# Seven block products for eight in the feed-forward down products of a two-block transformer kernel

## The chip, the cores and the metric

The kernel runs on one NeuronCore of a Trainium2 chip. The core has a matrix engine (TensorE, PE in the profile, with its weight loads as PEld), three engines for the rest (VectorE is DVE, ScalarE is ACT, GpSimd is POOL), and a SyncE queue (SP) that starts the transfers from HBM. The engines run their own instruction streams and meet at semaphores. The metric is the device time of one launch in microseconds, the median of the runs.

## The reference

Two layers of one transformer block, then one block of another kind, for 512 tokens of width 1024, in float32. The change lies in the feed-forward part of the first two layers:

```python
h2 = rms_norm(x, norm2[l])                                        # x: 512 x 1024
x = x + jnp.square(jax.nn.relu(h2 @ w_up[l])) @ w_down[l]         # w_up: 1024 x 4096, w_down: 4096 x 1024
```

In front of it in a layer stand a projection, four kinds of attention and an output projection. Behind the second layer comes a modulated block, whose modulation is the sum over k of `c[k] * w_ada[k, :]`, 3072 wide; VectorE forms it during the second layer's feed-forward part.

## The kernel before

**Precision.** TensorE takes float32 operands in a rounded format (float32r). Each operand is split into a high part (the rounded value) and a low part (value minus high part), and each product of two tiles is three matmuls, high x high, high x low, low x high (`three`, L2136 to L2138). A matmul takes a 128 x 128 stationary tile and a moving tile of 512 columns.

**Weights.** A job is 1024 rows by 512 columns of a weight matrix, in two halves ("pieces") of 512 x 512, 1 MB each. SP loads a piece into one of four `raw` slots, ScalarE copies it to `w_hi` (L1413), GpSimd subtracts to make `w_lo` in two instructions of 128 x 1024 (L1367). `w_hi` and `w_lo` have two slots: the piece after next can be split only when TensorE has finished with the slot.

**Feed-forward part.** The 4096 hidden columns come in four groups of 1024. A group has four jobs: two "up" jobs make the hidden values transposed (hidden feature on the partitions, 512 tokens along the free dimension) in the four PSUM banks G, a tile of 128 features in each; then two "down" jobs with the hidden values as stationary and a piece of `w_down` as moving operand make 512 tokens x 512 columns in G. A job is 96 matmuls, a half job 48; a group is 384. For each up tile ScalarE takes the relu out of PSUM (L1693), VectorE squares it (L2087), makes the high part (L2088) and the low part (L2089), all 128 x 512. For each down tile VectorE adds the bank, scaled by the inverse square norm `inv_square`, to X in SBUF (L2068). In the second layer VectorE also adds six parts of the modulation in a group (L2115, 128 x 1024 each). The loop over groups is a hardware loop on most engines, and each engine's order within it is written out by hand; nothing reorders an engine's instructions.

**Around it.** Before the first group the X rows are turned through the PSUM banks S and split; behind the last group the next layer's first job does the same. The S banks are free during the feed-forward part.

## Time and profile before

| | us |
|---|---|
| median of 3 runs (1829.14 to 1831.54) | 1830.73 |
| profiled execution, first to last instruction | 1830.6 |
| TensorE busy | 1790.4 |
| VectorE busy | 932.7 |
| GpSimd busy | 728.6 |
| ScalarE busy | 663.0 |

The profile covers one execution. Of its own time the record gives the span from the first to the last instruction, and nothing around it. Busy times are sums over an engine's instructions. Matmuls overlap in the pipeline, so their durations add up to more than the time that they need; the distance of their starts is the cost of one. In a timeline row the first number is the start in us, the second the duration; a bracket at the end says how long the engine stood idle before, and what ended that.

### The profile page before, as it was taken

How to read it: one execution, taken by the hardware profiler on the slowest of the kernel's cores; microseconds unless marked ns; L12 is line 12 of the kernel's file. 1: busy time of each engine (PE TensorE's matmuls, PEld its weight loads, DVE VectorE, ACT ScalarE, POOL GpSimd, SP SyncE). 2: the span in 40 equal slices, each digit the busy share in tenths (PEclk: the TensorE clock that was granted, in tenths of full speed). 3: DMA queues.
4: the chain of work that ended last, by engine and by line, in shares of the span. 5: the costliest groups of instructions: out<-in, count | busy, mean ns of one | idle time of the engine just before them, and what ended most of it. 6: DMA issues, size and time to landing. Idle time of an engine off the chain costs nothing.

```text
span 1830.6 us, 22975 instructions
## 1 busy us (share of the span) xinstructions
PE 1790.4 (98%) x9055; PEld 1461.3 (80%) x9057; DVE 932.7 (51%) x1500; ACT 663.0 (36%) x1234; POOL 728.6 (40%) x328
## 2 busy tenths in 40 slices
PE   8999899999999999999999999999999999999998
PEld 8677668888888886776688888888788988888786
DVE  4678752514232246797627362727522134339476
ACT  4543653312222245345523131222435343443213
POOL 4232434444444533333444444544343434224343
PEclk9999999999999999999999999999899999999999
DMA  7225002222232232220025524242232223222221
GB/s 233 70 69 172 2 24 92 93 92 92 95 111 92 69 98 97 69 70 1 24 69 185 179 97 161 92 161 96 93 133 86 70 75 116 87 69 92 93 69 46
DMA packets 105023, 171.00 MB, mean 93 GB/s; under 512 B 21679, under 2 KB 39495, under 8 KB 103784
## 3 DMA queue, kind: packets, MB, share of 16 engines
q1 hardware_dynamic: 103896, 169.79, 28.2%
q8 instruction: 60, 0.98, 0.2%
q14 instruction: 27, 0.22, 0.0%
q10 hardware_dynamic: 1040, 0.00, 0.0%
HBM read 166.56 MB, written 7.93 MB: 95 GB/s over the span
## 4 chain that ended last, share of the span: by engine, by line
PE 90%; DVE 6%; ACT 2%; issue 1%; DMA 0%; SPq 0%; DVEq 0%; ACTq 0%
PE G L2136 26%; PE G L2138 25%; PE G L2137 25%; PE S L2423 2%; PE S L1138 1%; DVE select L1976 1%; PE G L2459 1%; DVE work L1812 1%; DVE neg_max L2012 1%; PE S L2184 1%; PE S L1112 1%; DVE top L1811 1%; PE G L2407 1%; PE S L1123 1%; PE G L2440 1%
## 5 line engine op out<-in xcount | busy, mean ns | idle before, releaser
L1367 POOL TENSOR_TENSOR w_lo<-raw,w_hi 128x1024 fp32r<-128x1024 f32 (+2 forms) x268 | 658.5, 2478 | 976.1 <-ACT w_hi L1413 667.0
L2136 PE MATMUL G<-h_hi,w_hi 128*128 128x512 f32 x896 | 355.9, 397 | 1.9 <-DVE h_lo L888 1.9
L1413 ACT ACTIVATE w_hi<-raw 128x2048 fp32r<-128x2048 f32 (+1 forms) x94 | 178.9, 1903 | 492.7 <-PE G L2138 492.7
L2138 PE MATMUL G<-h_hi,w_lo 128*128 128x512 f32 x896 | 349.9, 391 | 0.0
L2137 PE MATMUL G<-h_lo,w_hi 128*128 128x512 f32 x896 | 349.7, 390 | 0.0
L2136 PE MATMUL G<-w_hi,h_hi 128*128 128x512 f32 (+2 forms) x704 | 277.2, 394 | 2.2 <-DVE h_lo L1765 1.2
L2138 PE MATMUL G<-w_hi,h_lo 128*128 128x512 f32 (+2 forms) x704 | 267.1, 379 | 0.0
L2137 PE MATMUL G<-w_lo,h_hi 128*128 128x512 f32 (+2 forms) x704 | 266.7, 379 | 0.0
L2136 PEld LDWEIGHTS G<-h_hi,w_hi 128*128 128x128 f32 x896 | 168.5, 188 | 39.2 <-issue 4.4
L2138 PE MATMUL G<-w_hi,u_lo 128*128 128x512 f32 x512 | 199.2, 389 | 0.0
L2136 PE MATMUL G<-w_hi,u_hi 128*128 128x512 f32 x512 | 199.2, 389 | 0.0
L2137 PE MATMUL G<-w_lo,u_hi 128*128 128x512 f32 x512 | 199.2, 389 | 0.0
L2138 PEld LDWEIGHTS G<-h_hi,w_lo 128*128 128x128 f32 x896 | 168.6, 188 | 36.2
L2137 PEld LDWEIGHTS G<-h_lo,w_hi 128*128 128x128 f32 x896 | 168.7, 188 | 34.6 <-issue 1.0
L2136 PEld LDWEIGHTS G<-w_hi,h_hi 128*128 128x128 f32 x704 | 140.1, 199 | 31.8 <-issue 11.9
L2138 PEld LDWEIGHTS G<-w_hi,h_lo 128*128 128x128 f32 x704 | 140.0, 199 | 21.2
L2137 PEld LDWEIGHTS G<-w_lo,h_hi 128*128 128x128 f32 x704 | 140.3, 199 | 20.3 <-issue 1.9
L2068 DVE SCALAR_TENSOR_TENSOR X<-G,inv_square,X 128x512 f32<-128x512 f32 x64 | 47.2, 749 | 210.5 <-PE G L2138 210.1
L2087 DVE TENSOR_TENSOR square<-relu 128x512 f32<-128x512 f32 x64 | 57.5, 899 | 158.1 <-ACT relu L1693 154.7
L722 ACT ACTIVATE w_hi<-raw 128x2048 fp32r<-128x2048 f32 x38 | 72.7, 1912 | 120.6 <-PE G L2138 120.6
L2138 PEld LDWEIGHTS G<-w_hi,u_lo 128*128 128x128 f32 x512 | 96.1, 188 | 20.0
L2137 PEld LDWEIGHTS G<-w_lo,u_hi 128*128 128x128 f32 x512 | 96.1, 188 | 20.0
(325 smaller groups left out, 2232.4 us busy)
## 6 DMA issues: line engine op xcount, KB each, us to landing
raw<-in_w_in_dram SPq DMA_DIRECT2D x40, 1024.0 KB, 5.2
raw<-in_w_up_dram SPq DMA_DIRECT2D x32, 1024.0 KB, 5.1
raw<-in_w_down_dram SPq DMA_DIRECT2D x32, 1024.0 KB, 5.0
raw<-in_w_out_dram SPq DMA_DIRECT2D x12, 1024.0 KB, 4.9
w_ada<-in_w_ada_dram SPq DMA_DIRECT2D x4, 3072.0 KB, 11.8
skew_scratch<-line_scratch SPq DMA_DIRECT2D x1, 4608.0 KB
raw<-in_w_in_dram SPq DMA_DIRECT2D x8, 512.0 KB, 4.1
raw<-in_w_in_dram SPq DMA_DIRECT2D x4, 832.0 KB, 6.6
```

Source lines behind the costliest of these rows:

```text
L722: act.activation(w_hi[:, c % SPLIT_SLOTS], raw[:, c % RAW_SLOTS], ACT.Copy).then_inc(high_ready, 1)
L1112: ins = pe.matmul(dst, queries[at, tile0 + n, q], keys[at, tile0 + n, k], start=True, stop=True)
L1123: ins = pe.transpose(S[:, 2 * (it % 2) + e, P * b:P * b + P], prob2[:, it % 2, e, P * b:P * b + P], ident)
L1138: ins = pe.matmul(dst, prob2[:, it % 2, e, P * place:P * place + P], values[:, m + 1 - blocks + b, HD * h:HD * h + HD], start=b == 0, stop ...
L1367: ins = pool.tensor_tensor(w_lo[:, c % SPLIT_SLOTS, part, 0:n], raw[:, c % RAW_SLOTS, part, 0:n], w_hi[:, c % SPLIT_SLOTS, part, 0:n].bitc ...
L1413: act.activation(w_hi[:, c % SPLIT_SLOTS, :, 0:n], raw[:, c % RAW_SLOTS, :, 0:n], ACT.Copy).then_inc(high_ready, 1)
L2068: dve.scalar_tensor_tensor(dst, G[:, t, :], factor, dst, ALU.mult, ALU.add).then_inc(bank_drained, 1)
L2087: step.done(dve.tensor_tensor(square[:], relu[:, n % 2, :], relu[:, n % 2, :], ALU.mult))
L2136: pe.matmul(dst, a_hi, b_hi, start=first, stop=False)
L2137: pe.matmul(dst, a_hi, b_lo, start=False, stop=False)
L2138: return pe.matmul(dst, a_lo, b_hi, start=False, stop=last)
L2423: pe.matmul(bank, qkT[at, p % 2, q, P * qt:P * qt + P], qkT[at, p % 2, k, P * tiles[0]:P * (qt + 1)], start=True, stop=False)
```

## The change

The product of a group, hidden (512 tokens x 1024) by down weights (1024 x 1024), is cut into 2 x 2 blocks (A11 to A22 of the hidden values with 256 tokens x 512 features, B11 to B22 of the weights with 512 x 512) and formed with seven block products in Winograd's form of Strassen's algorithm: A11·B11, A12·B21, S2·T2, S3·T3, S1·T1, S4·B22, A22·T4, with sums S1 = A21 + A22, S2 = S1 - A11, S3 = A11 - A21, S4 = A12 - S2 and four sums T of weight blocks. A product is 24 matmuls (two token tiles, four feature tiles, three each).

TensorE's order in groups 0 to 2 is A11, A12, S2, S3, U0, S1, U1, S4, A22, U2, U3, where U0 to U3 are the half jobs of the next group's up products; the last group has the seven products alone. The products use two bank pairs of S. A11, S2, S3 and A22 add up in the "long" pair, S1 and S4 in the short one (which A12 has before them); VectorE reads a pair after each product, 14 sums in a group, and the next product on that pair waits for it.

VectorE now makes the four S, two of the T (T2, T3), the low parts of the hidden blocks, and the low parts of the weights of five products, in place of square and high part. GpSimd makes the low parts of the up halves as before, those of S4's and A22's weights, and T1 and T4. ScalarE squares, makes all high parts (weights in halves of 128 x 1024). A fifth raw slot is added, and each slot's role moves from group to group. The modulation's weights come in 24 loads of 128 x 1024 into one buffer instead of four of 128 x 6144. The group loops are unrolled.

The core of the diff (removed lines are the group functions of the engines, told above):

```diff
+PRODUCTS = (("A11", "B11"), ("A12", "B21"), ("S2", "T2"), ("S3", "T3"), ("S1", "T1"), ("S4", "B22"), ("A22", "T4"))
+LONG_BANK = (True, False, True, True, False, False, True)
+READ_BEFORE = (P_A22, P_S4, P_A11, P_S2, P_A12, P_S1, P_S3)
+GOES_TO = ((0, 1, None), (0, 1, P_A11), (0, 0, None), (1, 0, None), (1, 0, P_S3), (0, 0, P_S2), (1, 1, None))
+def ffn_pieces():
+    order = [("U", 0, n) for n in range(4)]
+    for g in range(FFN_GROUPS):
+        more = g + 1 < FFN_GROUPS
+        for p in range(NP):
+            order.append(("P", g, p))
+            if more:
+                order += {P_S3: [("U", g + 1, 0)], P_S1: [("U", g + 1, 1)],
+                          P_A22: [("U", g + 1, 2), ("U", g + 1, 3)]}.get(p, [])
+    return order
...
 # SP, loads for group g during the products of g - 1
+                for g in range(1, FFN_GROUPS):
+                    sums = 2 * (l * FFN_GROUPS + g)
+                    wait_product_split(sp, l, g - 1, P_S2)
+                    sp.wait_ge(sum_made["T1"], sums)
+                    sp.wait_ge(sum_made["T4"], sums)
+                    load_up(g, 0)
+                    wait_product_split(sp, l, g - 1, P_S3)
+                    load_up(g, 1)
+                    load_modulation(1)
+                    wait_up_split(sp, l, g, 0)
+                    load_up(g, 2)
+                    wait_product_split(sp, l, g - 1, P_S1)
+                    load_up(g, 3)
+                    load_modulation(3)
+                    wait_up_split(sp, l, g, 1)
+                    load_down(g, "B11")
+                    wait_product_split(sp, l, g - 1, P_S4)
+                    load_down(g, "B12")
+                    load_modulation(1)
+                    wait_product_split(sp, l, g - 1, P_A22)
+                    load_down(g, "B22")
+                    wait_up_split(sp, l, g, 2)
+                    load_down(g, "B21")
+                    load_modulation(1)
...
 # GpSimd
+                    wait_product_split(pool, l, g, P_A11)
+                    weights_sum(g, "T1", role_slot(l, g, "B22"), role_slot(l, g, "B11"), t2_half)
+                    wait_product_split(pool, l, g, P_A12)
+                    weights_sum(g, "T4", role_slot(l, g, "B21"), role_slot(l, g, "B21"), t2_half)
+                    more = g + 1 < FFN_GROUPS
+                    if more:
+                        up_low(g + 1, 0)
+                        up_low(g + 1, 1)
+                    late_weight_low(g, P_S4)
+                    late_weight_low(g, P_A22)
+                    if more:
+                        up_low(g + 1, 2)
+                        up_low(g + 1, 3)
...
 # ScalarE
+                def products_high(g):
+                    at = lambda p: FFN_AT["P", g, p]
+                    more, last = g + 1 < FFN_GROUPS, l == DEPTH - 1
+                    up_tile(g, 1, 3)
+                    weight_half(at(P_A12), 0)
+                    block_high(g, "A12", 1)
+                    weight_half(at(P_A12), 1)
+                    block_high(g, "S2", 1)
+                    weight_high(at(P_S2))
+                    block_high(g, "A22")
+                    block_high(g, "S1")
+                    weight_high(at(P_S3))
+                    block_high(g, "S4")
+                    if more:
+                        up = lambda n: FFN_AT["U", g + 1, n]
+                        weight_high(up(0))
+                        weight_high(at(P_S1))
+                        weight_high(up(1))
+                        weight_high(at(P_S4))
                         for t in range(TT):
+                            up_tile(g + 1, 0, t)
+                        weight_high(at(P_A22))
+                        weight_high(up(2))
+                        first_blocks_high(g + 1)
+                        weight_high(up(3))
+                        second_blocks_high(g + 1)
+                        return
...
 # VectorE, group g
+                    more = g + 1 < FFN_GROUPS
+                    sums_s1_s2(g, 1)
+                    weight_low(g, P_A12, 0)
+                    block_low(g, "A12", 1)
+                    weight_low(g, P_A12, 1)
+                    take_sum(g, P_A11, 0)
+                    sum_s4(g)
+                    take_sum(g, P_A11, 1)
+                    block_low(g, "S2", 0)
+                    weight_low(g, P_S2, 0)
+                    block_low(g, "S2", 1)
+                    weight_low(g, P_S2, 1)
+                    take_sum(g, P_A12, 0)
+                    weight_low(g, P_S3, 0)
+                    take_sum(g, P_A12, 1)
+                    weight_low(g, P_S3, 1)
+                    block_low(g, "A22")
+                    if more:
+                        add_modulation(1)
+                    block_low(g, "S1")
+                    block_low(g, "S4")
+                    take_sum(g, P_S2, 0)
+                    if not more:
+                        weight_low(g, P_S1, 0)
+                    take_sum(g, P_S2, 1)
+                    if not more:
+                        weight_low(g, P_S1, 1)
+                    take_sum(g, P_S3, 0)
+                    if more:
+                        weight_low(g, P_S1, 0)
+                    take_sum(g, P_S3, 1)
+                    if more:
+                        weight_low(g, P_S1, 1)
+                        add_modulation(3)
+                    take_sum(g, P_S1, 0)
+                    take_sum(g, P_S1, 1)
+                    if more:
+                        add_modulation(1)
+                        for hh in range(2):
+                            sum_s3(g + 1, hh)
+                    take_sum(g, P_S4, 0)
+                    take_sum(g, P_S4, 1)
+                    if more:
+                        first_blocks_low(g + 1)
+                    take_sum(g, P_A22, 0)
+                    take_sum(g, P_A22, 1)
+                    if more:
+                        add_modulation(1)
+                        sum_t3(g + 1)
+                        sum_t2(g + 1)
+                        before_products(g + 1)
...
 # TensorE
+                def down_product(g, p):
+                    a = PRODUCTS[p][0]
+                    s = FFN_AT["P", g, p] % SPLIT_SLOTS
+                    hi, lo = high_of[a], low_of[a]
+                    for hh in range(2):
+                        wait_product_split(pe, l, g, p, hh)
+                        pe.wait_ge(act_low[a], blocks_upto(a, l, g) + (0 if a in WHOLE else hh) + 1)
+                        for r in range(2):
+                            bank = S[:, 2 * LONG_BANK[p] + r, :]
+                            if hh == 0:
+                                before = READ_BEFORE[p]
+                                if before < p:
+                                    wait_taken(pe, l, g, before, r)
+                                elif g:
+                                    wait_taken(pe, l, g - 1, before, r)
+                            at = slice(P * r, P * r + P)
+                            for kk in (2 * hh, 2 * hh + 1):
+                                ins = three(bank, hi[:, kk, at], lo[:, kk, at], w_hi[:, s, kk, :], w_lo[:, s, kk, :],
+                                            kk == 0 and (p == P_A11 or not LONG_BANK[p]) and p != P_S4,
+                                            kk == HALF_K - 1, p in CONTINUES)
```

`before_products(g)` makes the low parts of A11's weights, the first halves of S1 and S2 and the low part of A12's first half; it stands in front of group g, during U3. `weight_low`, `weight_half`, `up_low` and `late_weight_low` work on 128 x 1024, `sums_s1_s2` and `block_low` with a half on 128 x 512, whole blocks and `sum_s4` on 128 x 1024.

## Rows read from the trace of the kernel before

**Rows 1.** Part 1 of the page: busy us (share of the span) x instructions, by engine.
```profile
PE 1790.4 (98%) x9055; PEld 1461.3 (80%) x9057; DVE 932.7 (51%) x1500; ACT 663.0 (36%) x1234; POOL 728.6 (40%) x328
```

**Rows 2.** Stretch: us, PE, PEld, DVE, ACT, POOL busy, PEclk, DMA share, GB/s.
```profile
409.00:496.00 87.00, 87.00 (x386) 72.06 (x385) 26.09 (x32) 19.92 (x16) 39.58 (x17) 1.00 0.29 97
```

**Rows 3.** Timeline of TensorE and GpSimd in that layer: start us, duration us.
```profile
452.89 0.39 PE L2136 MATMUL G<-w_hi,u_hi 128*128 128x512 f32 x1
453.80 0.39 PE L2137 MATMUL G<-w_lo,u_hi 128*128 128x512 f32 x1
...
463.25 4.74 POOL L1367 TENSOR_TENSOR w_lo<-raw,w_hi 128x1024 fp32r<-128x1024 f32 x2 [6.13 <-ACT w_hi L1413]
474.13 4.75 POOL L1367 TENSOR_TENSOR w_lo<-raw,w_hi 128x1024 fp32r<-128x1024 f32 x2 [6.14 <-ACT w_hi L1413]
```

**Rows 4.** Groups of ScalarE by form: count | busy us, mean ns | idle before.
```profile
L1413 ACT ACTIVATE w_hi<-raw 128x2048 fp32r<-128x2048 f32 x90 | 172.5, 1916 | 492.7 <-PE G L2138 492.7
L1693 ACT ACTIVATE relu<-G 128x512 f32<-128x512 f32 x64 | 38.3, 599 | 114.0 <-PE G L2138 73.5 <-DVE u_lo L2089 40.5
L1413 ACT ACTIVATE w_hi<-raw 128x1680 fp32r<-128x1680 f32 x4 | 6.4, 1610 | 0.0
```

**Rows 5.** Timeline of VectorE in the first layer's feed-forward part.
```profile
440.68 0.69 DVE L2087 TENSOR_TENSOR square<-relu 128x512 f32<-128x512 f32 x1
441.41 0.43 DVE L2088 CAST u_hi<-square 128x512 fp32r<-128x512 f32 x1
...
453.17 0.75 DVE L2068 SCALAR_TENSOR_TENSOR X<-G,inv_square,X 128x512 f32<-128x512 f32 x1 [10.60 <-PE G L2138]
```

**Rows 6.** Timeline of GpSimd and VectorE in the second layer's feed-forward part.
```profile
1001.03 2.39 POOL L1367 TENSOR_TENSOR w_lo<-raw,w_hi 128x1024 fp32r<-128x1024 f32 x1 [6.25 <-ACT w_hi L1413]
1003.38 2.84 POOL L1367 TENSOR_TENSOR w_lo<-raw,w_hi 128x1024 fp32r<-128x1024 f32 x1
...
1001.06 2.91 DVE L2089 TENSOR_TENSOR u_lo<-square,u_hi 128x512 fp32r<-128x512 f32 x1
1003.90 3.41 DVE L2115 SCALAR_TENSOR_TENSOR ada_sum<-w_ada,c_col,ada_sum 128x1024 f32<-128x1024 f32 x1
1008.67 1.28 DVE L2115 SCALAR_TENSOR_TENSOR ada_sum<-w_ada,c_col,ada_sum 128x1024 f32<-128x1024 f32 x1
...
1033.11 4.75 POOL L1367 TENSOR_TENSOR w_lo<-raw,w_hi 128x1024 fp32r<-128x1024 f32 x2 [6.14 <-ACT w_hi L1413]
...
1033.90 0.75 DVE L2068 SCALAR_TENSOR_TENSOR X<-G,inv_square,X 128x512 f32<-128x512 f32 x1 [12.90 <-PE G L2138]
```

**Rows 7.** Stretches, columns as in rows 2 (PEclk is the granted clock).
```profile
205.00:217.00 12.00, 10.03 (x93) 7.70 (x91) 10.40 (x22) 7.75 (x23) 3.98 (x4) 1.00 0.01 1
853.00:860.00 7.00, 5.94 (x43) 4.82 (x44) 6.83 (x16) 3.51 (x13) 2.51 (x2) 0.76 0.01 2
...
1303.00:1310.00 7.00, 7.00 (x37) 5.12 (x36) 4.85 (x16) 1.79 (x7) 0.00 (x0) 0.72 0.00 1
...
1316.00:1320.00 4.00, 4.00 (x14) 3.06 (x13) 2.33 (x5) 2.65 (x3) 0.98 (x1) 0.57 0.89 305
1320.00:1323.00 3.00, 3.00 (x17) 2.43 (x16) 1.75 (x2) 0.78 (x1) 3.00 (x2) 1.00 0.00 0
```

**Rows 8.** Timeline of TensorE at its longest gaps inside the span.
```profile
209.18 0.33 PE L2459 MATMUL G<-probT,rows_v 128*64 128x128 f32 x2 [1.77 <-ACT mixT_da L1621]
...
854.06 0.66 PE L2459 MATMUL G<-probT,rows_v 128*64 128x128 f32 x8 [1.77 <-ACT mixT_da L1621]
...
1315.35 0.47 PE L2136 MATMUL G<-h_hi,w_hi 128*128 128x512 f32 x1 [1.88 <-DVE h_lo L888]
...
1317.25 0.63 PE L2136 MATMUL G<-h_hi,w_hi 128*128 128x512 f32 x1
1317.68 0.63 PE L2137 MATMUL G<-h_lo,w_hi 128*128 128x512 f32 x1
```

**Rows 9.** Transfers by line: count, KB each, median us from issue to landing.
```profile
raw<-in_w_up_dram SPq DMA_DIRECT2D x32, 1024.0 KB, 5.1
```

More of the change, by code:

```diff
@@ L351 @@
               JOB_D: (D_COLS,), JOB_V: (CV_COLS, DV_COLS)}
-def loads_upto(c):
-    parts = [len(PROJ_PARTS[x // 2]) if x // 2 < PROJ_JOBS else 1 for x in range(c + 1) if x % RAW_SLOTS == c % RAW_SLOTS]
-    return 16 * sum(parts)
 FIRST_GROUP_PIECE = 2 * FFN_JOB
-LOADS_TO_GROUPS = [loads_upto(FIRST_GROUP_PIECE - RAW_SLOTS + s) for s in range(RAW_SLOTS)]
-GROUP_LOADS = 16 * 2 * GROUP_JOBS // RAW_SLOTS
-LAYER_LOADS = [x + FFN_GROUPS * GROUP_LOADS for x in LOADS_TO_GROUPS]
+MORE_RAW = RAW_SLOTS
+ROLES = ("B11", "B12", "B22", "B21", "T2")
@@ new lines, with raw_slot, role_slot, up_slot @@
+RAW_ORDER, RAW_ROLES = raw_places()
+def raw_slot(l, c):
+    return RAW_ORDER[l][c % RAW_SLOTS]
+def role_slot(l, g, role):
+    return RAW_ROLES[FFN_GROUPS * l + g][role]
+def up_slot(l, g, n):
+    return RAW_ORDER[l][n] if g == 0 else role_slot(l, g - 1, ("T2", "B12", "T2", "B11")[n])
+def product_slot(l, g, p):
+    role = PRODUCTS[p][1]
+    return role_slot(l, g, {"T3": "B12", "T1": "B11", "T4": "B21"}.get(role, role))
+def ffn_loads(l):
+    order = [("U", 0, n) for n in range(4)] + [("B", 0, role) for role in ROLES[:4]]
+    for g in range(1, FFN_GROUPS):
+        order += [("U", g, n) for n in range(4)] + [("B", g, role) for role in ROLES[:4]]
+    return order
@@ new lines, in load_slot, with count_loads, add @@
+def load_slot(l, what):
+    kind, g, n = what
+    return up_slot(l, g, n) if kind == "U" else role_slot(l, g, n)
+def count_loads():
+    counts, at = [0] * (RAW_SLOTS + 1), {}
+    def add(key, slot, parts=1):
+        counts[slot] += 16 * parts
+        at[key] = counts[slot]
+    for l in range(DEPTH):
+        for c in range(FIRST_GROUP_PIECE):
+            add((l, c), raw_slot(l, c), len(PROJ_PARTS[c // 2]) if c // 2 < PROJ_JOBS else 1)
+        for what in ffn_loads(l):
+            add((l, what), load_slot(l, what))
+    for c in range(TOTAL_PIECES - PIECE0):
+        add((DEPTH, c), raw_slot(DEPTH, c))
+    return at
@@ L1277, in _ @@
                 for c in range(FIRST_GROUP_PIECE):
-                    job, half, slot = c // 2, c % 2, c % RAW_SLOTS
-                    slot_free(number + (c + 1))
+                    job, half, slot = c // 2, c % 2, raw_slot(l, c)
+                    if l and c < RAW_SLOTS:
+                        wait_raw_free(sp, l - 1, c)
+                    else:
+                        slot_free(number + (c + 1))
                     if job < PROJ_JOBS:
@@ L2121, in _, with first_blocks_low @@
+                def first_blocks_low(g):
+                    for a in ("A11", "S3"):
+                        for hh in range(2):
+                            block_low(g, a, hh)
+                if last:
                     dve.wait_ge(c_loaded, 16)
@@ L2508, in _ @@
+                for kind, g, n in FFN_ORDER:
+                    (up_half if kind == "U" else down_product)(g, n)
             second_tensor(pe, three, product, in_rows, in_columns, turn)
```

605 lines of the change are left out of this document (422 added, 183 removed).

## The prediction

> **What bounds the kernel now.** The page first: TensorE is busy for 98% of the span, no other engine for more than 51% (weight loads, PEld, overlap the matmuls) [rows 1]. A stretch of 87 us, one feed-forward group of the first layer, has TensorE busy without a gap, VectorE 26 us, ScalarE 20 us, GpSimd 40 us [rows 2]. Busy time misleads as a cost of one matmul: the records last 390 ns, but overlap; the starts are 0.227 us apart [rows 3]. GpSimd's splits, one for each half job of 48 matmuls, start 10.88 us apart, which is 48 x 0.2267. A group of 8 half jobs is therefore 87.04 us [rows 3]. TensorE waits for nothing there [rows 2], so a matmul taken away is worth 0.2267 us, as long as the other engines keep up with the shorter products.
>
> **What is removed.** A group's down products need 7 x 24 = 168 matmuls for 192: 24 x 0.2267 = 5.44 us less, for 8 groups 43.5 us. Nothing else in the change gives time. A product now lasts 5.44 us, its halves 2.72 us, and what the old order had 10.88 us for must be done in that.
>
> **What the other engines get.** Their prices:
> - VectorE, both inputs in SBUF: 0.69 us for 512 wide when undisturbed [rows 5]. 1024 wide is not shown for a subtraction; it lies between the 1.28 us of a three-operand instruction [rows 6] and, at the least, 2 x 0.43 of a cast; I take 1.25, next to the same kind of operands. 0.05 between two.
> - Taking a sum from PSUM: 0.75 [rows 5].
> - ScalarE: 1.92 for 2048 wide and 1.61 for 1680 [rows 4] make 0.83 ns a column and 0.22 fixed, so 1.07 for 1024 and 0.64 for 512; a relu from PSUM 0.60 [rows 4].
> - GpSimd: 4.74 for two of 1024 [rows 3], so 2.37 each. A signal between engines: about 0.1.
>
> In a group VectorE gave 8 x (0.69 + 0.43 + 0.69) = 14.5 us of such work and 6.0 of sums. Now: ten halves of weight low parts, four of T2 and T3 and four whole blocks (S4; the low parts of A22, S1, S4) at 1.25, and six S halves and eight low halves at 0.69, together 32 us, and 14 sums, 10.5 us. In the second layer 6 modulation parts, as before. GpSimd keeps 16 pieces: eight of up weights, four late low parts, T1 and T4: 38 us.
>
> The sum of VectorE, 43 us in 81.6, fits. But the two engines exclude one another, and the trace shows how [rows 6]. The low part started at 1001.06 takes 2.91 us, because GpSimd runs to 1003.42; GpSimd's next one, 2.84 for 2.37, waits for that low part; the modulation at 1003.90 takes 3.41 for 1.28, because GpSimd has the turn again. A sum from PSUM at 1033.90 in the middle of a GpSimd piece takes its 0.75: only work with all its inputs in SBUF is shut out. So each GpSimd piece inside a queue of VectorE's costs that queue what is left of the piece.
>
> **The path: VectorE's queue between the last up half and the third sum.** Zero is the end of U3, the products have ideal starts A11 0, A12 5.44, S2 10.88, S3 16.32, U0 21.76. S3 adds into the banks of S2, so its first matmul waits for the first sum of S2 (READ_BEFORE), and that sum stands on VectorE behind everything listed here.
> - ScalarE: relu and square of the last tile end at 1.45, then half a weight of A12 (2.55), A12's second half (3.2), the other weight half (4.3).
> - VectorE: S1 and S2 halves 1.55 to 2.97; weight low 4.3; A12 low 5.04; weight low 6.35. Product A12 needs these at 5.44 and 8.16: no stall. Sum of A11, 7.15.
> - At 6.45 GpSimd begins T4 (it waits for the A12 weight split) and holds until 8.8. S4 on VectorE runs 8.85 to 10.1; second sum of A11 10.95; T4's second piece 10.1 to 12.5 shuts out the low part of S2. Then low 13.2, weight 14.5, low 15.25, weight 16.55.
> - So S2 starts at 14.6 instead of 10.88, and ends at 20.05.
> - VectorE goes on: sum of A12 17.35, weight of S3 18.65, sum 19.45, weight 20.75, A22 low 22.05, S1 low 23.35. The load of U0 is issued when the weights of S2 are split, 16.6, and lands 5.1 us later [rows 9]; ScalarE 22 to 23.05; GpSimd wants its piece at 23.1, gets it at 23.35 and holds until 25.7. S4 low 26.95, first sum of S2 27.75.
> - S3 starts at 27.85 instead of 16.32: 11.5 us late, two idle gaps of TensorE, 3.7 and 7.8.
>
> In groups 0 to 2 of the second layer a modulation part stands behind A22's low part: 1.25 and one more GpSimd piece in front of S4's low part: S3 starts at 31.35, 15.0 late. In group 3 no up half follows, and GpSimd is out of the way: S3 starts at 25.5, 9.2 late, and 0.75 more for its second bank, whose sum waits behind half a weight split: 9.9. In the second layer two products with the gain stand there too, 1.7: 11.6. Sum: 3 x 11.5 + 9.9 + 3 x 15.0 + 11.6 = 101.0 us.
>
> Behind S3 there is slack. U0's low parts are ready 4 us ahead. S1 and S4 have an up half of 10.88 in front of them. A22 gets its first half 0.4 ahead. U2's second half is about even: GpSimd has A22 and U2 back to back, while VectorE puts low parts of the next A11 between; between 0 and 1.2 late, I take 0.6, for 6 groups 3.6 us. In the second layer SP's queue stands on the modulation's single buffer until VectorE has used it (three loads in a row between its U3 and B11 loads), but the next load behind it, B11, is wanted only after U3's split, some 30 us on. At the layer's end the sums in PSUM take 0.75 after the last matmul, as now: nothing.
>
> **The clock.** TensorE's clock fell where it had little to do: in 1303 to 1310, among thin matmuls, 0.72 was granted (it has two levels, 1.2 and 2.4 GHz, so over half of the time at the lower one), and behind a gap of 1.88 the matmuls start 0.43 apart instead of 0.227 [rows 7, 8]; 1316 to 1320 has 0.57, so 0.86 of those 4 us at the lower level, 3.4 us [rows 7]. Slow work of 3.4 to 4 us, say 3.7, loses 3.7 x (1 - 0.227/0.428) = 1.74 us. Around a gap of 1.77 that ends at 854.06, 0.76 was granted in 7 us; around the same gap, ended at 209.18, 1.00 [rows 7, 8]: so a fall after a gap is not certain. I take one of 1.74 for each S3 gap, 8 x 1.74 = 13.9; a slow S2 costs nothing, since VectorE is later anyway. Without any it is 0; with twice the length 28.
> The Trainium skill ("TensorE: Matmul & The Clock Gate", section "HAM oscillation — how this bites in real kernels") says that a wait which recurs in each round of the loop lets every round start at the lower clock. The rows leave this open, by them alone one could enter nothing or a half; so by the rule the sum is the one below, by the rows alone down to 14 us less.
>
> **Sum.** -43.5 + 101.0 + 3.6 + 13.9 = +75.0 us. The profiled execution took 1830.6 us between first and last instruction, the runs' median is 1830.73: the same. 1830.6 + 75 = 1905.6, I say **1906 us**, own range 1890 to 1925.
>
> **Rivals.**
> - *The pieces of GpSimd fall beside VectorE's queue.* The order of work leaves T4 and U0 free to come a few us earlier or later. Without the lock the queue is 5 x 0.69 + 10 x 1.25 + 5 x 0.75 and 19 gaps, 20.7 us; from 1.55 on S2's first sum ends at 22.2, S3 starts at 22.3, still 6.0 late; with the same additions as above 3 x 6.0 + 6.75 + 3 x 7.25 + 8.45 = 55.0. 1830.6 - 43.5 + 55.0 + 13.9 = 1856; without a fall of the clock 1842. For it: T4 comes from a wait, its start may slip. Against it: T4's wait is the very weight split that VectorE ends, so it falls in the queue by itself. Chance 0.19.
> - *The clock stays down longer,* for all of S3 and half of U0, about 11 us at half rate each time: 11 x 0.47 = 5.2 us for 1.74, and U2 late by 1.2: 1906 + 8 x 3.4 + 4 = 1937. For it: low grants from 1303 to 1320; against it: the full grant right behind, with dense work [rows 7]. Chance 0.12.
> - *The queue is short enough: faster.* The place is the same wait of S3 for the first sum of S2, the price is the 1024-wide instruction. If it goes at the cast's rate (0.86) and the lock doesn't strike, the ten save 3.9 us, S3 starts at 18.4, 2.1 late; 8 x 2.1 + 3 x 1.25 and 3.2 of the groups 3 = 24; 1830.6 - 43.5 + 24 = 1811. It decides from the point where S3 starts before 21.76, 5.44 behind the ideal. Against it: 0.69 for the two-input form, 0.43 for the cast alone [rows 5]. Chance 0.10.
> - Between these, at 1827 to 1834: chance 0.04. Forecast: 0.55.
>
> **Numbers.** A difference under 0.2% (3.7 us) is about what can't be told from none. Slower 0.55 + 0.19 + 0.12 = 0.86, same 0.04, faster 0.10. The range leaves out the two cases that aren't slower, 0.14, and half of the slow-clock case, 0.06: from the lower end of the first rival, 1842, to 1930.
>
> **What would show it.** 192 matmuls fewer, and TensorE idle before the first matmul of S3 in each group, 5 to 11 us, ended by VectorE's sum; a shorter gap before S2, ended by its low parts; both in all 8 groups, longest in the second layer's first three. VectorE's 1024-wide subtractions at 1.25 where GpSimd rests and 2.5 to 3.6 where it runs. Granted clock under 1 behind the gaps. I am wrong if S3 follows S2 without a gap, or if gaps stand before up halves.

## The result, and the profile after

The changed kernel takes 1883.66 us (median of 4 runs, 1881.34 to 1885.56), the kernel before beside it 1831.13 (1829.14 to 1833.9): a ratio of 1.0292, 95% interval 1.0276 to 1.0308. So it is slower, as forecast, and 22 us less slow than the 1906 that stood there: within the range of 1842 to 1930, below the 1890 to 1925 that the forecast itself had. The profiled span is 1883.8 against 1830.6, 53.2 more.

Part 1 of the page of the changed kernel answers to [rows 1]:

```profile
PE 1780.6 (95%) x8863; PEld 1441.2 (77%) x8865; DVE 1105.1 (59%) x1612; ACT 815.3 (43%) x1498; POOL 743.7 (39%) x328
```

The 192 matmuls are gone (9055 to 8863), and TensorE is idle for 103 us where it was idle for 40. Where it waits is read from the timeline of TensorE, rows with an idle time in the bracket: in the first layer's first group ahead of S2 and of S3, and in the second layer's first group ahead of A11 and of S3 (shorter ones, of 1.96 and 1.88 us, stand there ahead of A12 and S2):

```profile
367.34 0.50 PE L2633 MATMUL S<-w_hi,s_high 128*128 128x512 f32 x1 [2.32 <-DVE w_lo L2506]
376.83 0.47 PE L2633 MATMUL S<-w_hi,s_high 128*128 128x512 f32 x1 [2.12 <-DVE X L2535]
...
1022.81 0.80 PE L2633 MATMUL S<-w_hi,a_high 128*128 128x512 f32 x1 [13.63 <-DVE w_lo L2506]
...
1052.51 0.77 PE L2633 MATMUL S<-w_hi,s_high 128*128 128x512 f32 x1 [4.91 <-DVE X L2535]
```

The first two are the pair that was forecast: S2 waits for VectorE's low part of its weights, S3 for the first sum of S2 (X). They stand in every group, but in the first layer's groups 0 to 2 they are 2.3 and 2.1 us, not 3.7 and 7.8; in the others 1.9 to 3.4 and 2.5 to 4.9. The third was not forecast. Stretches of the same kernel, columns as in [rows 2]:

```profile
354.00:383.00 29.00, 24.56 (x100) 19.53 (x99) 23.58 (x23) 14.46 (x17) 10.95 (x4) 0.94 0.29 82
...
1009.00:1061.00 52.00, 29.62 (x99) 22.85 (x99) 38.37 (x34) 18.41 (x25) 17.57 (x6) 0.77 0.33 101
1121.00:1154.00 33.00, 26.28 (x101) 20.75 (x100) 26.19 (x26) 14.57 (x18) 12.65 (x5) 0.90 0.33 101
```

In 354 to 383 the kernel before had 29.00 us of TensorE at clock 1.00. The second layer loses more, and with the clock at 0.77 and 0.90.

The lengths of the groups come from the starts of their first A11 matmul. An ideal group is 87.04 - 5.44 = 81.6 us, the last one of a layer 7 x 5.44 = 38.1.

| | measured excess | forecast |
|---|---|---|
| first layer, groups 0 to 2 | 7.0 each (353.98, 442.60, ...: 88.6 apart) | 11.5 + 0.6 + 1.74 = 13.8 each |
| first layer, group 3 | 9.3 (619.80 to 667.22) | 9.9 + 1.74 = 11.6 |
| second layer, group 0 | 30.8 (1009.02 to 1121.39) | 15.0 + 0.6 + 1.74 = 17.3 |
| second layer, groups 1 and 2 | 11.5 and 11.1 | 17.3 each |
| second layer, group 3 | 10.8 | 11.6 + 1.74 = 13.3 |
| elsewhere | 2.1 (1.7 ahead of the first group, 0.4 between the layers) | 0 |
| matmuls | -43.5 | -43.5 |
| sum | +53.1 (the spans: +53.2) | +75 |

VectorE and GpSimd from A11's first matmul (353.98) on, where the forecast had laid out its queue:

```profile
359.70 0.75 DVE L2535 SCALAR_TENSOR_TENSOR X<-S,inv_square,X 128x512 f32<-128x512 f32 x1
360.36 3.00 DVE L2473 TENSOR_TENSOR hidden<-hidden,s_sum 128x1024 f32<-128x1024 f32 x1
363.39 0.75 DVE L2535 SCALAR_TENSOR_TENSOR X<-S,inv_square,X 128x512 f32<-128x512 f32 x1
364.06 2.09 DVE L2498 TENSOR_TENSOR s_low<-s_sum,s_high 128x512 fp32r<-128x512 f32 x1
366.08 1.21 DVE L2506 TENSOR_TENSOR w_lo<-raw,w_hi 128x1024 fp32r<-128x1024 f32 x1
367.21 0.68 DVE L2498 TENSOR_TENSOR s_low<-s_sum,s_high 128x512 fp32r<-128x512 f32 x1
367.81 1.21 DVE L2506 TENSOR_TENSOR w_lo<-raw,w_hi 128x1024 fp32r<-128x1024 f32 x1
...
372.54 1.21 DVE L2498 TENSOR_TENSOR a_low<-hidden,a_high 128x1024 fp32r<-128x1024 f32 x1
373.67 1.21 DVE L2498 TENSOR_TENSOR s_low<-hidden,s_high 128x1024 fp32r<-128x1024 f32 x1
374.81 1.21 DVE L2498 TENSOR_TENSOR s_low<-hidden,a_high 128x1024 fp32r<-128x1024 f32 x1
375.94 1.39 DVE L2535 SCALAR_TENSOR_TENSOR X<-S,inv_square,X 128x512 f32<-128x512 f32 x2
...
359.86 5.74 POOL L1669 TENSOR_TENSOR raw<-raw 128x1024 f32<-128x1024 f32 x2 [8.21 <-DVE w_lo L2506]
375.40 5.21 POOL L1651 TENSOR_TENSOR w_lo<-raw,w_hi 128x1024 fp32r<-128x1024 f32 x2 [9.79 <-ACT w_hi L1766]
```

The reader sees three things. T4 (L1669) falls into the queue where it was put, at 5.9 us after A11's start (forecast 6.45), and shuts out S4 (3.00 for 1.21) and the first low part of S2 (2.09 for 0.68), but not the sum from PSUM at 363.39 (0.75 as always). U0's piece (L1651) comes at 375.40, after VectorE's last low part has begun, so its lock strikes nothing that S3 waits for. And where nothing shuts VectorE out, its instructions start 1.13 and 0.60 us apart, less than the 1.21 and 0.68 that they are recorded with; the forecast had 1.30 and 0.74.

### The profile page after: what moved, and what is told of

It is laid out like the page before. It is cut to its first block, busy times and chain, and to the rows that moved or that the text cites. A ratio compares the mean times of both kernels' runs of the same rounds, so it can differ in the third digit from the quotient of the medians.

```text
span 1883.8 us, 22625 instructions
## 1 busy us (share of the span) xinstructions
PE 1780.6 (95%) x8863; PEld 1441.2 (77%) x8865; DVE 1105.1 (59%) x1612; ACT 815.3 (43%) x1498; POOL 743.7 (39%) x328
## 4 chain that ended last, share of the span: by engine, by line
PE 72%; DVE 16%; POOL 4%; issue 3%; ACT 3%; DMA 1%; SPq 1%; DVEq 0%; ACTq 0%
PE G L2633 18%; PE G L2635 18%; PE G L2634 18%; POOL w_lo L1651 3%; DVE w_lo L2506 2%; PE S L2633 2%; PE S L2634 2%; PE S L2635 2%; PE S L2921 2%; DVE hidden L2473 2%; POOL w_lo L1660 2%; DVE s_low L2498 1%; PE S L1344 1%; DVE X L2535 1%; DVE select L2349 1%
## 5 line engine op out<-in xcount | busy, mean ns | idle before, releaser
L1616 POOL TENSOR_TENSOR w_lo<-raw,w_hi 128x1024 fp32r<-128x1024 f32 (+2 forms) x140 | 335.2, 2415 | 581.5 <-ACT w_hi L930 297.2
L1766 ACT ACTIVATE w_hi<-raw 128x1024 fp32r<-128x1024 f32 x140 | 144.1, 1052 | 269.3 <-PE G L2635 154.8
L1651 POOL TENSOR_TENSOR w_lo<-raw,w_hi 128x1024 fp32r<-128x1024 f32 x52 | 138.9, 2693 | 184.7 <-ACT w_hi L1766 184.7
L2535 DVE SCALAR_TENSOR_TENSOR X<-S,inv_square,X 128x512 f32<-128x512 f32 x112 | 82.4, 744 | 111.4 <-PE S L2635 110.8
L2633 PE MATMUL S<-w_hi,s_high 128*128 128x512 f32 x192 | 84.8, 442 | 45.6 <-DVE X L2535 24.3
L2633 PE MATMUL S<-w_hi,a_high 128*128 128x512 f32 x256 | 101.7, 397 | 16.4 <-DVE w_lo L2506 15.6
L2635 PE MATMUL S<-w_hi,s_low 128*128 128x512 f32 x256 | 106.7, 417 | 0.0
L1632 POOL TENSOR_TENSOR prob<-prob,inv_sum 128x256 f32<-128x256 f32 (+3 forms) x48 | 60.1, 1253 | 106.8 <-DVE inv_sum L2390 106.4
L2634 PE MATMUL S<-w_lo,a_high 128*128 128x512 f32 x256 | 101.1, 395 | 0.0
```

The costliest lines, as they stand in the source:

```text
L1616: ins = pool.tensor_tensor(w_lo[:, c % SPLIT_SLOTS, part, 0:n], raw[:, raw_slot(l, c), part, 0:n], w_hi[:, c % SPLIT_SLOTS, part, 0:n].bit ...
L1632: pool.tensor_tensor(part, part, inverse, ALU.mult).then_inc(prob_scaled, 1)
L1651: pool.tensor_tensor(w_lo[:, f % SPLIT_SLOTS, part], raw_at(up_slot(l, g, n))[:, part], w_hi[:, f % SPLIT_SLOTS, part].bitcast(F32), ALU.s ...
L1766: act.activation(w_hi[:, f % SPLIT_SLOTS, part], piece_source(l, FFN_ORDER[f])[:, part], ACT.Copy).then_inc(ffn_high, 1)
L2535: dve.scalar_tensor_tensor(X[:, t, at], S[:, 2 * LONG_BANK[p] + r, :], inv_square[:, t:t + 1], X[:, t, at], ALU.mult, ALU.add).then_inc(su ...
L2633: pe.matmul(dst, a_hi, b_hi, start=first, stop=False, skip_group_check=more)
```

## The experiments

My theory: the two gaps come from the order of VectorE's queue and from T4's lock on it, and the second layer adds its modulation. Rivals: VectorE has too much work in this stretch whatever its order; the clock is what costs; the second layer's excess is something else. Times of before beside these runs lie between 1829.3 and 1830.7; ratios are to them.

**1. The sums of S2 ahead of the low parts of S1, A22 and S4.**

```diff
                     weight_low(g, P_S3, 1)
+                    take_sum(g, P_S2, 0)
+                    take_sum(g, P_S2, 1)
+                    block_low(g, "S1")
...
                     block_low(g, "A22")
...
-                    block_low(g, "S1")
                     block_low(g, "S4")
-                    take_sum(g, P_S2, 0)
...
-                    take_sum(g, P_S2, 1)
```

> The two sums of S2 are taken ahead of the low parts of A22, S1 and S4 (and the modulation part) on VectorE; all work stays. If VectorE's order sets the start of S3 (my theory), the gap of TensorE before S3 goes in all eight groups: 2.1 us in groups 0 to 2 of the first layer, 3.7 in its group 3, 4.9, 3.3, 3.4 and 2.5 in the second, together 25 us with the 0.8 before the last group's second product: about 1859 us, gaps before S2 as they are. If S3 waits for something else (its own weights, its low part, the lock), less than 5 us come back and a gap stays before S3.

Measured 1857.60 us (1855.32 to 1861.55), ratio 1.0147 [1.0130, 1.0164], 26 us less than the change. TensorE's timeline in the first group, ahead of S2, S3 and the two halves of U0:

```profile
366.56 0.50 PE L2632 MATMUL S<-w_hi,s_high 128*128 128x512 f32 x1 [2.31 <-DVE w_lo L2506]
372.63 0.47 PE L2632 MATMUL S<-w_hi,s_high 128*128 128x512 f32 x1 [0.34 <-DVE X L2535]
378.85 0.50 PE L2632 MATMUL G<-h_hi,w_hi 128*128 128x512 f32 x1 [0.49 <-POOL w_lo L1651]
382.15 0.49 PE L2632 MATMUL G<-h_hi,w_hi 128*128 128x512 f32 x1 [1.63 <-POOL w_lo L1651]
```

The gap before S3 is 0.34 for 2.12, and at most 0.34 in every group: it was the queue. The one before S2 is untouched, and U0, reached earlier, now waits for its low parts on GpSimd. So the sums' place in the queue is shown as the cause; but a third limit stands 2 us behind it.

**2. T4 thin.** The two instructions, their waits and signals stay, at 16 columns for 512; the rest of T4 is left unformed.

```diff
-                        pool.tensor_tensor(raw_at(place)[:, part], raw_at(minuend)[:, part],
-                                           raw_at(role_slot(l, g, "T2"))[:, part], ALU.subtract)
+                        cols = slice(0, 16 if name == "T4" else 512)
+                        pool.tensor_tensor(raw_at(place)[:, part, cols], raw_at(minuend)[:, part, cols],
+                                           raw_at(role_slot(l, g, "T2"))[:, part, cols], ALU.subtract)
```

> GpSimd's two pieces for T4 work on 16 columns of 512 instead of all (the rest of T4 is left unformed), so they hold GpSimd a few tenths of a us. If the exclusion of the two engines costs VectorE's queue what the trace shows there (1.8 us at the S4 sum, 1.4 us at the low part of S2), the queue ends 3.2 us earlier: the 2.3 us gap before S2 goes, S3 still starts late, and about 3 us a group come back, 20 to 27 us in all: about 1860 us. If the pieces cost nothing (VectorE is late by its own work alone), the time stays within 5 us and the S4 sum keeps 3.0 us.

Measured 1861.08 us (1859.33 to 1862.91), ratio 1.0167 [1.0150, 1.0184], 23 us less than the change. No group of the first layer has a gap before S2 any more, and the second layer's have 0.3 us or less; the only one left in the first group:

```profile
373.17 0.47 PE L2635 MATMUL S<-w_hi,s_high 128*128 128x512 f32 x1 [3.16 <-DVE X L2537]
```

S2 starts in time and ends earlier, VectorE's queue has the same length behind it, so the gap before S3 grows from 2.12 to 3.16. The lock of T4's pieces is shown as the cause of the gap before S2, of all of it in the first layer.

**3. The modulation spread.** In the second layer two parts of the modulation stand ahead of the first group instead of six, none between A22's and S1's low parts, the others between other work of VectorE; the loads follow.

```diff
                 sum_t3(0)
-                add_modulation(2)
+                add_modulation(1)
...
                 sum_t2(0)
-                add_modulation(3)
                 before_products(0)
...
                     block_low(g, "A22")
-                    if more:
-                        add_modulation(1)
```

> Five of the modulation's 24 parts leave the stretch in front of the second layer's first product and the part behind A22's low part leaves the queue; they are put, one at a time, where VectorE stands idle (seven in a group, one in the last). If VectorE's waits for the single buffer's transfers cause the 13.6 us gap before the second layer's first A11, and the part in the queue the rest of what the second layer loses more than the first, the gap goes with the slow clock behind it and groups 0 to 2 lose 7 us each as in the first layer: about 32 us less, 1852 us. If the gap comes from something else at the layer's start (the loads of the weight blocks, the late T1), no more than 5 us come back.

Measured 1866.56 us (1865.06 to 1871.40), ratio 1.0209 [1.0190, 1.0227], 17 us less than the change, half of what I expected. Ahead of it, VectorE in the changed kernel at the second layer's start:

```profile
1003.61 1.28 DVE L2461 SCALAR_TENSOR_TENSOR ada_sum<-w_ada,c_col,ada_sum 128x1024 f32<-128x1024 f32 x1 [3.67 <-DMA w_ada<-in_w_ada_dram]
...
1015.60 1.28 DVE L2461 SCALAR_TENSOR_TENSOR ada_sum<-w_ada,c_col,ada_sum 128x1024 f32<-128x1024 f32 x1 [3.62 <-DMA w_ada<-in_w_ada_dram]
1020.34 1.28 DVE L2461 SCALAR_TENSOR_TENSOR ada_sum<-w_ada,c_col,ada_sum 128x1024 f32<-128x1024 f32 x1 [3.46 <-DMA w_ada<-in_w_ada_dram]
1021.54 2.35 DVE L2506 TENSOR_TENSOR w_lo<-raw_more,w_hi 128x1024 fp32r<-128x1024 f32 x2
```

A11's weights (1021.54) stand behind parts whose loads go one at a time through a single buffer. And TensorE in this experiment, ahead of A12, S2 and S3 of the same group:

```profile
1011.70 0.50 PE L2635 MATMUL S<-w_hi,a_high 128*128 128x512 f32 x1 [1.84 <-DVE w_lo L2507]
1020.92 0.50 PE L2635 MATMUL S<-w_hi,s_high 128*128 128x512 f32 x1 [3.47 <-DVE w_lo L2507]
1030.41 0.47 PE L2635 MATMUL S<-w_hi,s_high 128*128 128x512 f32 x1 [2.14 <-DVE X L2536]
```

The 13.63 us are gone (the 1.84 ahead of A12 stood there before, as 1.96), and S3 starts 9.5 us behind S2 in groups 0 to 2 where it was 10.7. So group 0 has an excess of 10.9 us for 30.8. But groups 1 to 3 have 12.4, 11.4 and 13.7 for 11.5, 11.1 and 10.8, and the wait ahead of S2 is 3.5 us in all four, where the first layer has 2.3. That is why half of the gain is missing. The trace of the changed kernel shows where this wait comes from. VectorE and GpSimd ahead of the second group of the first layer (A11 at 442.60):

```profile
428.09 1.40 DVE L2535 SCALAR_TENSOR_TENSOR X<-S,inv_square,X 128x512 f32<-128x512 f32 x2
...
438.65 0.69 DVE L2473 TENSOR_TENSOR hidden<-hidden 128x512 f32<-128x512 f32 x1 [2.36 <-ACT hidden L1999]
...
436.37 5.22 POOL L1669 TENSOR_TENSOR raw<-raw,raw_more 128x1024 f32<-128x1024 f32 x2 [8.76 <-DVE w_lo L2506]
```

The same ahead of the second group of the second layer (A11 at 1121.39):

```profile
1106.88 1.40 DVE L2535 SCALAR_TENSOR_TENSOR X<-S,inv_square,X 128x512 f32<-128x512 f32 x2
1108.20 1.27 DVE L2461 SCALAR_TENSOR_TENSOR ada_sum<-w_ada,c_col,ada_sum 128x1024 f32<-128x1024 f32 x1
...
1117.44 1.88 DVE L2473 TENSOR_TENSOR hidden<-hidden 128x512 f32<-128x512 f32 x1 [1.16 <-ACT hidden L1999]
1119.36 2.77 DVE L2473 TENSOR_TENSOR s_sum<-hidden 128x512 f32<-128x512 f32 x1
...
1116.37 5.21 POOL L1669 TENSOR_TENSOR raw<-raw,raw_more 128x1024 f32<-128x1024 f32 x2 [9.96 <-DVE w_lo L2506]
```

The sums of A22 (X) start 14.5 us ahead of A11 in both layers. Behind them the second layer has a part of the modulation (1108.20), and what follows is 1.2 us later: T1 on GpSimd starts 5.0 us ahead of A11 for 6.2, and shuts out S1's first half (1.88 for 0.69) as well as S2's. So S2 starts 14.4 us after A11 instead of 13.4. This run left that part where it was and put a second one between T3 and T2: T1 starts 2.4 us ahead of A11 there (1094.33 for 1096.77), and S2 15.4 us after it. So this excess, too, comes by the rows from the modulation's place in the queue, from a part that the run did not take out; no run took that part alone away.

**4. Work for TensorE in the gaps.** Ahead of S2 and S3 TensorE multiplies masks of 128 x 128 into a bank that is free, 18 times in the first layer and 28 in the second, so that it is idle for less of the gaps.

```diff
+                    if p in (P_S2, P_S3):
+                        pe.wait_ge(bank_drained, unit + (TT * (FFN_JOB + UP_JOBS * (g + 1)) + UNITS_CREDIT))
+                        keep_going(18 if l == 0 else 28)
```

> TensorE turns the identity tile 18 times (28 in the second layer) before S2 and before S3, into a PSUM bank that is free then, about 2 and 3 us of the gaps, so that the clock has no reason to fall; nothing else changes. By my step (a slow S2 costs nothing, since VectorE is later anyway) the first layer keeps its time within 1 us although its clock stays full, and the second gains only what ran slow behind S3, 5 to 8 us: 1876 to 1880. If each fall of the clock is paid for in time, 1.7 us or more for each of the eight groups and both layers, 14 us or more come back: 1870 or less.

Measured 1877.45 us (1876.42 to 1879.39), ratio 1.0260 [1.0243, 1.0277], 6 us less. Its timeline of TensorE in the first layer, S3 in the first group and in the next:

```profile
373.73 2.13 PE L2710 MATMUL G<-masks 128*128 128x128 f32 x18
377.63 0.47 PE L2633 MATMUL S<-w_hi,s_high 128*128 128x512 f32 x1 [1.78 <-DVE X L2535]
...
466.25 0.47 PE L2633 MATMUL S<-w_hi,s_high 128*128 128x512 f32 x1 [1.76 <-DVE X L2535]
```

The granted clock in 354 to 383 is now 1.00 for 0.94, no matmul there starts 0.43 apart, and the group is as long as it was: 466.25 - 377.63 = 88.62, against 465.44 - 376.83 = 88.61. A slow S2 costs nothing in the first layer's groups 0 to 2, since VectorE ends S3's wait. What was won lies, by the two traces, where the fall had come in S3, behind which nothing is late: 2.3 us in the first layer's last group, 2.9 and 2.2 in the second layer's groups 0 and 1. The S3 of the first of these, in the changed kernel, then here:

```profile
642.00:649.00 7.00, 6.37 (x16) 5.11 (x17) 3.41 (x4) 0.81 (x1) 0.00 (x0) 0.54 0.52 107
```

```profile
642.00:649.00 7.00, 5.42 (x23) 4.19 (x24) 5.00 (x6) 1.06 (x1) 0.92 (x1) 1.00 0.50 87
```

A fall at that place is not certain from one trace to the next: in the trace of run 3, whose first layer is the same and has no filler, this S3 has none either. And the filler leaves two falls in the second layer, behind A11 of the first group and in S3 of the third (0.72 granted in 1231 to 1237). So the work in the gaps gives back about 6 us in all, where 13.9 was put for the clock.

**5. T4 on VectorE, behind S2's weights; the sums of S2 ahead of those of A12.** The low parts of S1, S4 and A22 follow behind, in that order; `TAKEN_AT` tells the waiting engines the new order of the sums.

```diff
+TAKEN_AT = (0, 2, 1, 3, 4, 5, 6)
...
-                    wait_product_split(pool, l, g, P_A12)
-                    weights_sum(g, "T4", role_slot(l, g, "B21"), role_slot(l, g, "B21"), t2_half)
...
                     weight_low(g, P_S2, 1)
+                    sum_t4(g)
+                    weight_low(g, P_S3, 0)
+                    take_sum(g, P_S2, 0)
+                    weight_low(g, P_S3, 1)
+                    take_sum(g, P_S2, 1)
                     take_sum(g, P_A12, 0)
-                    weight_low(g, P_S3, 0)
                     take_sum(g, P_A12, 1)
-                    weight_low(g, P_S3, 1)
+                    block_low(g, "S1")
...
```

> T4 is formed by VectorE behind S2's weights instead of by GpSimd, and the two sums of S2 are taken ahead of those of A12, with the low parts of S1, S4 and A22 behind them. By my reading (the lock of T4's two pieces makes the gap before S2, the queue behind it the gap before S3): the gap before S2 is gone in all eight groups, the one before S3 is under 1 us, each worth what the run with the thin T4 and the run with the sums first took off (about 23 and 26 us); what comes back is U0 or A12 1 to 2 us late in six groups, and the 13.6 us at the start of the second layer stay. So 1840 to 1850 us. By the rival that VectorE simply has too much work in this stretch, so that any order only moves the wait: T4's two sums of 1.2 us add to it, the time that leaves S2 and S3 stands before A12, U0 or A22, and the time is 1860 us or more.

Measured 1858.64 us (1856.65 to 1860.18), ratio 1.0151 [1.0135, 1.0167]: a miss. Both gaps are gone (at most 0.3 us is left of either in groups 0 to 2), and the gains of 1 and 2 (26 and 23 us) don't add up: 25 us is all. TensorE ahead of the two halves of U0, then GpSimd, ScalarE and SP's queue in that group:

```profile
379.61 0.50 PE L2639 MATMUL G<-h_hi,w_hi 128*128 128x512 f32 x1 [2.51 <-POOL w_lo L1652]
382.92 0.50 PE L2639 MATMUL G<-h_hi,w_hi 128*128 128x512 f32 x1 [1.65 <-POOL w_lo L1652]
...
375.56 7.31 POOL L1652 TENSOR_TENSOR w_lo<-raw,w_hi 128x1024 fp32r<-128x1024 f32 x2 [22.97 <-ACT w_hi L1765]
...
374.42 2.01 ACT L1765 ACTIVATE w_hi<-raw 128x1024 fp32r<-128x1024 f32 x2 [6.35 <-DMA raw<-in_w_up_dram]
...
369.14 14.13 SPq L1544 DMA_DIRECT2D raw<-in_w_up_dram  x3
```

U0 is wanted at 377.10. Its load, issued when S2's weights are split, lands at 374.4 here as in the changed kernel (ScalarE splits it at 374.26 there), and GpSimd's two pieces then take 7.31 us beside VectorE's low parts. That is the third limit that 1 showed: a group is 87.0 us (377.10 to 464.10) for 88.6, ideal 81.6. The number came out near the rival's ("1860 or more"), and U0 is one of the places that it named; but U0 waits for a load and for GpSimd's pieces, and not for VectorE's amount of work, as the next run shows, which has the same work in another order, with U0 behind S1.

**6 and 7. Reordered, with T4 on VectorE and with T4 on GpSimd.** Both build on the order of 5: S1 with its weights ahead of U0, the sums of A12 behind S1's low part, and the modulation's parts moved (six in a row behind S1's sums, two ahead of the first group). They differ in T4 alone.

```diff
-                order += {P_S3: [("U", g + 1, 0)], P_S1: [("U", g + 1, 1)],
+                order += {P_S1: [("U", g + 1, 0), ("U", g + 1, 1)],
...
+                    block_low(g, "S1")
                     take_sum(g, P_A12, 0)
-                    weight_low(g, P_S3, 0)
+                    weight_low(g, P_S1, 0)
                     take_sum(g, P_A12, 1)
-                    weight_low(g, P_S3, 1)
+                    weight_low(g, P_S1, 1)
+                    block_low(g, "S4")
                     block_low(g, "A22")
...
+                    add_modulation(6 if more else 1)
```

> As the kernel with T4 on VectorE, and besides S1's product stands ahead of both first up halves, and the parts of the modulation are spread so that two stand before the second layer's first group instead of six in a row behind a single buffer. By my reading: no gap above 1 us inside any of the eight groups, none of 13 us at the start of the second layer, and TensorE at full clock through both layers, so 1830.7 - 43.5 + 0 to 20 for what stays: 1790 to 1808 us, faster than before the change. By the rival that VectorE has too much work whatever the order: 1830 us or more. By the rival that the second layer's excess is not the modulation but something that falls only there: the gaps of the second layer stay and the time is about 1820 us.

> As the reordered kernel, but T4 stays on GpSimd where the change put it. By my reading the lock of T4 is then the one thing left: a gap of 2 to 3.5 us before S2 in each of the eight groups and 15 to 25 us more than the reordered kernel, some 1812 to 1826 us. If the place of T4 does not matter once the queue is in order, the two are within 4 us of each other.

With T4 on VectorE: 1823.08 us (1822.23 to 1824.78), ratio 0.9960 [0.9947, 0.9974], 7.6 us less than the kernel before beside it. With T4 on GpSimd: 1850.43 us (1847.21 to 1854.25), ratio 1.0101 [1.0082, 1.0119]. The same 87 us of the first layer, first with T4 on VectorE, then on GpSimd:

```profile
330.00:417.00 87.00, 86.91 (x383) 71.41 (x382) 56.84 (x49) 44.93 (x58) 38.86 (x16) 1.00 0.29 98
```

```profile
330.00:417.00 87.00, 84.69 (x366) 69.34 (x366) 53.63 (x45) 44.06 (x57) 40.37 (x17) 0.98 0.28 90
```

And the row that makes the difference, in the second of them:

```profile
366.98 0.50 PE L2624 MATMUL S<-w_hi,s_high 128*128 128x512 f32 x1 [2.31 <-DVE w_lo L2507]
```

With T4 on VectorE TensorE has no gap in groups 0 to 2 of the first layer (82.2 us each, ideal 81.6), with VectorE busy for 56.8 us of 87, against 53.6 with T4 on GpSimd: "too much work whatever the order" is refuted there. T4 on GpSimd costs 27 us, 3.4 a group, for which 15 to 25 were expected: the gap of 2.31 in the first layer, up to 3.5 in the second, and the clock behind it. My range for 6 (1790 to 1808) was too good by 15 us at the least, and with it the one for 7 (1812 to 1826). What stays in 6 is a gap at S4 in the first layer's last group, and in the second layer one ahead of A12 in each group (1.8 us in the first, 2.3 in the others):

```profile
632.94 0.77 PE L2630 MATMUL S<-w_hi,a_high 128*128 128x512 f32 x1 [5.31 <-DVE X L2541]
...
1082.90 0.50 PE L2630 MATMUL S<-w_hi,a_high 128*128 128x512 f32 x1 [2.29 <-DVE w_lo L2505]
```

The time is near the 1820 of the rival that looked for the second layer's excess elsewhere. But ahead of 1082.90 VectorE takes the modulation's parts in a row and waits 3.4 to 3.8 us for the load of each (1030.75 to 1053.47), so that the sums of A22 and A11's low parts come late: what stays there is still the modulation.

**8. A second round of order on top of 6.** In a layer's last group A22's low part goes behind sums; of the six modulation parts in a row two, and the one ahead of T3, go between other work.

```diff
-                    block_low(g, "A22")
+                    if more:
+                        block_low(g, "A22")
                     take_sum(g, P_S3, 0)
                     take_sum(g, P_S3, 1)
                     take_sum(g, P_S1, 0)
+                    if not more:
+                        block_low(g, "A22")
                     take_sum(g, P_S1, 1)
-                    add_modulation(6 if more else 1)
+                    add_modulation(4 if more else 1)
...
+                        add_modulation(1)
+                        sum_s3(g + 1, 1)
```

> The reordered kernel with two more moves in VectorE's order: in a layer's last group the sums that free S4's bank stand ahead of A22's low part, and four parts of the modulation instead of six stand in one row, the others between the blocks of the next group. By my reading the gap of 5.3 us before S4 in the first layer's last group shrinks by the 3.4 us of A22's low part, and the 2.3 us before A12 in three groups of the second layer, with the half clock behind them, go away, since VectorE waits there 3.4 to 3.8 us for each load of the modulation and the work of the next group then stands in those waits: 1808 to 1816 us, against 1823 for the reordered kernel. If the parts of the modulation are bound by their loads alone and all end at the same time as before, the second layer stays as it is and the time is 1818 to 1821 us.

Measured 1814.97 us (1812.55 to 1815.91), ratio 0.9912 [0.9899, 0.9926], the fastest of all. TensorE at S4 of the first layer's last group, and what has come in the second layer ahead of U0, in place of the wait before A12:

```profile
629.26 0.47 PE L2635 MATMUL S<-w_hi,a_high 128*128 128x512 f32 x1 [2.02 <-DVE X L2541]
...
1049.15 0.50 PE L2635 MATMUL G<-h_hi,w_hi 128*128 128x512 f32 x1 [1.05 <-POOL w_lo L1652]
```

The gap of 5.31 is 2.02, 3.3 us less: the low part that was moved had taken 3.37 there beside GpSimd's pieces. The time is within the range expected, below the 1818 to 1821 of the case that the parts are bound by their loads alone. The distance of the span to 1787.1 (1830.6 - 43.5) is still 26 us; U0's low parts in the second layer and the starts and ends of the layers are in it. I did not follow it further.

## Why the prediction was right, and where its sizes were off

- **The gain** of 43.5 us held: 192 matmuls, 0.2267 us apart.
- **The path** held: S2 late for T4's lock, S3 late for S2's sum behind VectorE's queue, in all eight groups; no gap ahead of an up half, and only one of 0.24 us inside U1 in the second layer's groups 0 to 2. Runs 1, 2 and 7 against 6 show each cause by itself.
- **Its size was off, by two terms.** In the first layer the excess was 30.4 us for 53.2 forecast. S2 started 13.4 us after A11 for 14.6 forecast, S3 22.9 for 27.9, that is 6.5 late instead of 11.5. The first term is VectorE's instruction: 1.25 + 0.05 and 0.69 + 0.05 were put, 1.13 and 0.60 apart is measured, 0.15 less for each. The nine from S2's start to S2's first sum (seven of these and two sums, 0.66 apart for 0.80) make 1.4; S2's own start was 1.2 early, by the same price and because T4 began 0.6 sooner. The second is U0's piece on GpSimd. It was put 0.25 us ahead of the queue's last low part, holding it for 2.35; with the queue that much shorter, it came after it (375.40 against 374.81), and cost nothing. Together 1.2 + 1.4 + 2.35 make the 5.0. So one small wrong price tipped a collision that was forecast by a margin of a quarter of a microsecond; the rival in which the pieces fall beside the queue had S3 6.0 late, nearer to the measured 6.5 than the forecast's 11.5. That rival was half true: U0 fell beside it, T4 did not. (Its 1856 leaves out the 3.6 us of U2; with them it is 1860.)
- **The clock** was put at 1.74 for each group, with "a slow S2 costs nothing". It did fall, but in the first layer's groups 0 to 2 in S2 and not in S3, and there it cost nothing. In S3 it fell in the first layer's last group and in three of the second layer; against starts 0.2267 apart the matmuls lost 2.7, 2.7, 1.6 and 1.3 us there, 8.3 in all for the 13.9, and run 4 gives back 6. The Trainium skill ("TensorE: Matmul & The Clock Gate", section "HAM oscillation — how this bites in real kernels") has a recurring wait start each round at the lower clock: the trace agrees that it recurs (matmuls 0.43 apart from 368.69 to 371.68, and so in S2 or S3 of each group of the first layer), and shows that its price is nothing where another engine is the later one.
- **The second layer** came out near its sum (64.2 for 65.4), but by two errors that cancel. Groups 1 to 3 were 11.1 each on the mean where 16.0 was put, for the reasons above, and because the modulation's part behind A22's low part cost 1.2 us alone, without the GpSimd piece that was added to it (2.25); the part ahead of T3, which was put at nothing, cost 1.1 through T1. The 30.8 of group 0 hold 13.8 that the prediction had not looked at: the six parts of the modulation ahead of the first group, each behind a load of 3.8 us into one buffer (run 3). The prediction's sentence on that buffer asked only for SP's next load, not for VectorE, which waits with all of its queue behind it. That the total lies as near as 22 us is luck in part: without these 13.8 it would have been some 1870, nearer to the rival's 1856 than to 1906.
- **U2** was put 0.6 late in six groups; U2 and U3 together were 0.4 late, so that held.
- **The lock** itself held: 3.00 and 2.09 for 1.21 and 0.68 beside T4. The Trainium skill ("SBUF — State Buffer", section "Who interferes with whom") has a VectorE instruction with two inputs in SBUF contend with a GpSimd one that reads SBUF, and one with at most one such input, outside VectorE's 2-port modes, not. The trace agrees: the sum from PSUM at 363.39, in the middle of T4, takes its 0.75.

## What to carry to other kernels

A change that halves the time of each step on the bound engine is priced by the queues of the others: lay out the next engine's queue in order, with starts rather than durations, and ask at each step what else it could do later. Here the same seven products go from 1884 to 1815 us by the order of the queues and the place of T4, with the same work. Of these 69 us, 27 come from giving T4 (2.35 us of VectorE's time in each group) to the engine that already has more to do, because its lock cost more than its work. When one wait is removed, look for what is only a little earlier than it: two gaps whose removal was worth 26 and 23 us alone were worth 25 together, for U0's load landed no earlier and GpSimd's pieces stood behind it.

## What the runs showed of the hardware that was not expected

- VectorE's next instruction starts up to 0.08 us ahead of the recorded end of the one before: 128x1024 recorded 1.21, starts 1.13 apart (372.54, 373.67, 374.81); 128x512 recorded 0.68, the next 0.60 behind it (367.21, 367.81). The forecast's sum over durations and gaps was 0.15 too much for each.
- A pair of GpSimd's pieces is stretched too: T4's took 5.74 us where a pair takes 4.74 in [rows 3], with S4, begun 0.5 us behind T4's first piece and recorded 3.00, ending in the middle of it. The records fit VectorE getting one instruction in between the two pieces.
- The lower clock doesn't begin at the gap's end: S2's matmuls at 367.34 to 368.69 start 0.23 to 0.34 apart, and only those from 368.69 to 371.68 0.43. With 18 thin matmuls (2.13 us) in these gaps the stretch has 1.00 (run 4).
